# The first MLP's second projection: eight of its sixteen blocks in three rounded products instead of full-precision ones

## The reference, cut to what matters

```python
# first layer, behind its mixer; D_MODEL = 1024, D_FF = 4096
h = _rmsnorm(x, norm_g[0, 1]) * (1.0 + scale_f) + shift_f
x = x + gate_f * (jnp.square(jax.nn.relu(h @ w_fc1[0])) @ w_fc2[0])
# second layer: norm, then the S5 mixer (a linear state-space recurrence
# whose kernels come from lam, log_step, b, c), its gated projections, its MLP
```

## Time and profile before

| | us |
|---|---|
| median of 3 runs | 1177.98 |
| lowest and highest run | 1172.93, 1179.79 |
| span of the profiled execution (first to last instruction) | 1171.0 |
| PE busy in it | 1112.6 (95%) |
| DVE busy | 816.0 (70%) |
| ACT busy | 557.7 (48%) |
| `fc2_0` in it, first to last product | 306.7 to 443.3 |

### The profile page before, as it was taken

One profiled execution on the slowest core, in us unless ns is written; L12 is line 12 of the kernel. 1 busy time (PEld: TensorE's weight loads), 2 busy tenths in 40 slices (PEclk: granted clock), 3 DMA queues, 4 the chain that ended last, 5 costly groups with the idle time before them and its releaser, 6 DMA issues.

```text
span 1171.0 us, 22089 instructions
## 1 busy us (share of the span) xinstructions
PE 1112.6 (95%) x9466; PEld 995.9 (85%) x9466; DVE 816.0 (70%) x1390; ACT 557.7 (48%) x876; POOL 44.6 (4%) x71
## 2 busy tenths in 40 slices
PE   6899898999999997879999999999999999999998
PEld 4778686988888885469999999999988899988898
DVE  1599466877578674875666654478899966659955
ACT  3224633445111124554555543356568846467944
POOL 0010001000000000000000000000000000042000
PEclk8999999999999998999999999989989999999999
DMA  9887688899848957865355555525433345343342
GB/s 369 356 280 269 250 323 315 305 339 328 335 182 258 342 186 165 323 245 184 140 184 182 183 189 185 187 81 180 145 109 114 130 153 177 131 153 117 108 145 72
DMA packets 38290, 246.46 MB, mean 210 GB/s; under 512 B 4400, under 2 KB 5584, under 8 KB 9648
## 3 DMA queue, kind: packets, MB, share of 16 engines
q1 hardware_dynamic: 29072, 182.36, 45.7%
q0 software_dynamic: 6240, 43.94, 10.0%
q10 hardware_dynamic: 2880, 18.74, 3.9%
HBM read 225.24 MB, written 19.79 MB: 209 GB/s over the span
## 4 chain that ended last, share of the span: by engine, by line
PE 78%; DVE 10%; DMA 5%; ACT 5%; issue 2%; SPq 0%; ACTq 0%; DVEq 0%
PE ps L1452 16%; PE ps L1454 15%; PE ps L1456 15%; PE ps L1459 10%; PE ps L1555 4%; DMA ca_dram<-more 2%; PE ps L1648 1%; PE ps L1528 1%; PE ps L2083 1%; PE ps L1601 1%; PE ps L1539 1%; PE ps L1534 1%; DMA more<-in_ada_w 1%; DVE ring_rounded L2229 1%; DMA ada_more<-in_ada_w 1%
## 5 line engine op out<-in xcount | busy, mean ns | idle before, releaser
L1452 PE MATMUL ps<-sq_rounded,w_high_rounded 128*128 128x256 f32 x1184 | 341.6, 288 | 2.5 <-DVE mixT_rounded L2236 1.3
L1456 PE MATMUL ps<-sq_rounded,ring_rounded 128*128 128x256 f32 x1184 | 336.2, 284 | 0.0
L2229 DVE TENSOR_TENSOR ring_rounded<-ring,w_high_rounded 128x1024 fp32r<-128x1024 f32 x220 | 260.6, 1226 | 92.1 <-ACT w_high_rounded L844 91.8
L1454 PE MATMUL ps<-hT_rounded,w_high_rounded 128*128 128x256 f32 x992 | 282.1, 284 | 0.0
L844 ACT ACTIVATE w_high_rounded<-ring 128x1024 fp32r<-128x1024 f32 x220 | 219.8, 1049 | 67.0 <-PE ps L1456 66.3
L1452 PEld LDWEIGHTS ps<-sq_rounded,w_high_rounded 128*128 128x128 f32 x1184 | 228.5, 193 | 11.0 <-issue 6.7
L1456 PEld LDWEIGHTS ps<-sq_rounded,ring_rounded 128*128 128x128 f32 x1184 | 228.6, 193 | 0.0
L1454 PEld LDWEIGHTS ps<-hT_rounded,w_high_rounded 128*128 128x128 f32 x992 | 191.8, 193 | 0.1
L1452 PE MATMUL ps<-more_rounded,w_high_rounded 128*128 128x256 f32 x448 | 127.4, 284 | 0.4 <-issue 0.3
L1456 PE MATMUL ps<-more_rounded,ring_rounded 128*128 128x256 f32 x448 | 126.8, 283 | 0.0
L1459 PE MATMUL ps<-big,ring 128*128 128x256 f32 x544 | 121.0, 381 | 0.0
(11 more groups left out here) (426 smaller groups left out, 1640.3 us busy)
## 6 DMA issues: line engine op xcount, KB each, us to landing
ring<-in_blocks SPq DMA_DIRECT2D x139, 1024.0 KB, 4.9
ada_w<-in_ada_w POOLq DMA_DIRECT2D x27, 1024.0 KB, 7.7
ada_more<-in_ada_w POOLq DMA_DIRECT2D x13, 1024.0 KB, 7.6
we_dram<-we_t ACTq DMA_DIRECT2D x8, 1024.0 KB, 8.3
ca_dram<-more ACTq DMA_DIRECT2D x8, 1024.0 KB, 11.9
ring<-we_dram SPq DMA_DIRECT2D x8, 1024.0 KB, 5.5
ring<-ca_dram SPq DMA_DIRECT2D x8, 1024.0 KB, 6.8
big<-in_ada_w SPq DMA_DIRECT2D x4, 1024.0 KB, 10.9
```

The costliest lines, as they stand in the source:

```text
L1452: nc.tensor.matmul(out, high[:, k, columns], x_high, start=start, stop=False, skip_group_check=True)
L1454: nc.tensor.matmul(out, high[:, k, columns], x_low, start=False, stop=False, skip_group_check=True)
L1456: last = nc.tensor.matmul(out, low[:, k, columns], x_high, start=False, stop=stop, skip_group_check=True)
L2229: nc.vector.tensor_tensor(rounded(w), w, w_high[:, c % 2, ks], ALU.subtract)\
```

## The change

Blocks k = 0 and 1 of every output unit become split blocks, and the first unit takes its blocks in the order k = 2, 3, 0, 1, so the split ones are j = 2, 3, 4, 5, 8, 9, 12, 13. ACT rounds the first 16 tiles of `hid` (eight activations of 128x512) and the eight blocks; DVE makes the rest of both. Since `w_high` is now used until block 13, the loads of the first two near tables move from SP to ACT, behind three of the four squares of the next norm. The diff, cut to its core:

```diff
-    phase("fc2_0", [("fc2_0", k, n) for n in range(4) for k in range(4)])
+    phase("fc2_0", [("fc2_0", k, n) for n in range(4) for k in FC2_ORDER[n]])
...
+FC2_ORDER = ((2, 3, 0, 1), (0, 1, 2, 3), (0, 1, 2, 3), (0, 1, 2, 3))
+FC2_ROUND_BEHIND = {3: 4, 4: 5, 5: 6, 7: 8}
+FC2_SPLIT = tuple(4 * n + i for n in range(4) for i in range(4) if FC2_ORDER[n][i] < 2)
...
         def hid0_high(t, count):
+            return (sq if t < DT else hT)[:, t % DT:t % DT + count]
...
             def load_near(n):            # SP's
                 sp.wait_ge(k_stored, 16 * (n + 1))
-                if n >= 2:
-                    sp.wait_ge(near_here[n - 2], 16 * L)
+                sp.wait_ge(near_here[n - 2], 16 * L)
...
-                if b in NEAR_AT:
-                    load_near(NEAR_AT.index(b))
...
+            def load_near(n):            # ACT's
+                act.wait_ge(blocks_done, first_block["fc2_0"] + FC2_SPLIT[n - 2] + 1)
+                for j in range(L):
+                    act.dma_start(s5_near[n][GC * j:GC * j + GC], ...).then_inc(near_here[n], 16)
...
+            for t in range(8):                                   # ACT, behind fc1_0
+                act.wait_ge(hid_ready, t + 1)
+                round_tiles(hid0_high(2 * t, 2), hid[:, 2 * t:2 * t + 2])
+            round_to(first_block["fc2_0"] + FC2_SPLIT[1] + 1)
             store_kernels(1)
             store_outputs(2)
             for m in range(3, 8):
...
                 copy_weights(m, (0, 1, 2, 3))
                 store_weights(m)
+                if m == 3:
+                    round_to(first_block["fc2_0"] + FC2_SPLIT[2] + 1)
                 store_kernels(m - 1)
                 store_outputs(m)
+                if m in FC2_ROUND_BEHIND:
+                    round_to(first_block["fc2_0"] + FC2_SPLIT[FC2_ROUND_BEHIND[m] - 1] + 1)
...
-            norm_stats(2, 2)
+            log_and_exp()
+            act.wait_ge(blocks_done, first_block["fc2_0"] + FC2_SPLIT[-2] + 1)
+            for p in range(3):
+                square(2, 2, p)
+            load_near(0)
+            load_near(1)
+            square(2, 2, 3)
+            norm_rstd(2)
...
             for n in range(4):                                   # PE
-                project_deep("fc2_0", n, 4, (hid,), ..., after_block)
+                project_deep("fc2_0", n, 4, hid_tile, hid_arrived, after_block, FC2_ORDER[n])
...
             s5_outputs(2)                                        # DVE
+            for t in range(8):
+                lower_tiles("fc2_0", t, hid[:, 2 * t:2 * t + 2], hid0_high(2 * t, 2))
+            lower_to(first_block["fc2_0"] + FC2_SPLIT[1] + 1)
             for m in range(3, 8):
                 s5_weights(m)
+                if m == 3:
+                    lower_next()
                 s5_outputs(m)
+                if m in (3, 4, 5):
+                    lower_next()
                 if m in (4, 6):
                     residual("fc2_0", gate_f, m // 2 - 2, m // 2 - 1)
+            lower_to(first_block["fc2_0"] + FC2_SPLIT[7] + 1)
             residual("fc2_0", gate_f, 2, 3)
             s5_kernels(7)
```

More of the change, by code:

```diff
@@ L198 @@
 W_OUT_SPLIT = (1, 2)
+FC2_ORDER = ((2, 3, 0, 1), (0, 1, 2, 3), (0, 1, 2, 3), (0, 1, 2, 3))
+FC2_ROUND_BEHIND = {3: 4, 4: 5, 5: 6, 7: 8}
+FC2_SPLIT = tuple(4 * n + i for n in range(4) for i in range(4) if FC2_ORDER[n][i] < 2)
 TOGETHER = 2
 QUARTERS = 4
-SPLIT_LO = {"w_in": "vector", "w_out": "vector", "fc1_0": "vector", "glu": "vector", "fc1_1": "vector", "fc2_1": "vector", "xbc": "vector", "z": "vector",
+SPLIT_LO = {"w_in": "vector", "w_out": "vector", "fc1_0": "vector", "fc2_0": "vector", "glu": "vector", "fc1_1": "vector", "fc2_1": "vector", "xbc": "vector", "z": "vector",
             "ssm_out": "vector", "ple_gate_0": "vector", "q": "vector", "gate": "vector",
             "attn_out": "vector", "ple_gate_1": "vector"}
-SPLIT_SETS = (("w_in", 8), ("w_out", 8), ("fc1_0", 8), ("glu", 4), ("fc1_1", 8), ("fc2_1", 16), ("xbc", 8), ("ssm_out", 16), ("ple_gate_0", 8), ("q", 8),
+SPLIT_SETS = (("w_in", 8), ("w_out", 8), ("fc1_0", 8), ("fc2_0", 8), ("glu", 4), ("fc1_1", 8), ("fc2_1", 16), ("xbc", 8), ("ssm_out", 16), ("ple_gate_0", 8), ("q", 8),
               ("attn_out", 8), ("ple_gate_1", 8))
@@ L223, in split_plan @@
         for b in range(start, end) if name in SPLIT_LO else ():
-            if b - start not in {"w_in": W_IN_SPLIT, "w_out": W_OUT_SPLIT}.get(name, range(end - start)):
+            if b - start not in {"w_in": W_IN_SPLIT, "w_out": W_OUT_SPLIT, "fc2_0": FC2_SPLIT}.get(name, range(end - start)):
                 continue
@@ L236, in program @@
     laid_out = {b: i for i, b in enumerate(from_inputs(plan))}
-    NEAR_AT = (first_block["fc2_0"] + 10, first_block["fc2_0"] + 11)
     ctx = ExitStack()
@@ L636, in program, with hid0_high @@
         head_sq2, at = carve(ada_w_flat, at, 4, T)
+        def hid0_high(t, count):
+            return (sq if t < DT else hT)[:, t % DT:t % DT + count]
         hid_high, _ = carve(more, 0, FT, T)
@@ L895, in norm_squares @@
                     square(i, version, p)
+            def load_near(n):
+                act.wait_ge(blocks_done, first_block["fc2_0"] + FC2_SPLIT[n - 2] + 1)
+                for j in range(L):
+                    act.dma_start(s5_near[n][GC * j:GC * j + GC],
+                                  k_dram[n].rearrange("(q c) x a -> c q (x a)", q=4)
+                                  [0:GC, :, 4 * (L - 1 - j) * GC:4 * (L - 1 - j) * GC + 4 * P]).then_inc(near_here[n], 16)
             def norm_rstd(i):
@@ L1500, in project_tokens, with project_deep @@
                 last.then_inc(blocks_done, 1)
-            def project_deep(phase, n, kblocks, x, arrived=None, after=None):
+            def project_deep(phase, n, kblocks, tile, arrived=None, after=None, order=range(4)):
                 ps = pair(start_unit(phase, n))
-                for kb in range(kblocks):
-                    block_products(phase, n * kblocks + kb,
+                for j, kb in enumerate(order):
+                    block_products(phase, n * kblocks + j,
                                    (lambda k: arrived(kb * KB + k)) if n == 0 and arrived else None,
-                                   [(k, ps[:, i], slice(P * i, P * i + P), at_tile(x, kb * KB + k),
-                                     kb == 0 and k == 0 and i == 0, kb == kblocks - 1 and k == KB - 1)
+                                   [(k, ps[:, i], slice(P * i, P * i + P), tile(kb * KB + k),
+                                     j == 0 and k == 0 and i == 0, j == kblocks - 1 and k == KB - 1)
                                     for k in range(KB) for i in range(2)])
                     if after:
-                        after(n * kblocks + kb)
+                        after(n * kblocks + j)
             def swept(phase, n, unit=None):
@@ L1837, in after_block, with hid_tile, hid_arrived @@
                     s5_kernels(S5_KERNEL_AT.index(16 + j))
+            def hid_tile(t):
+                if t < 2 * KB:
+                    return rounded(hid0_high(t, 1)[:, 0]), rounded(hid[:, t])
+                return hid[:, t]
+            def hid_arrived(t):
+                if t % 2:
+                    return
+                if t < 2 * KB:
+                    pe.wait_ge(a_low, SET_BASE["fc2_0"] + t // 2 + 1)
+                else:
+                    pe.wait_ge(hid_ready, t // 2 + 1)
             for n in range(4):
-                project_deep("fc2_0", n, 4, (hid,), lambda k: pe.wait_ge(hid_ready, k // 2 + 1) if k % 2 == 0 else None,
-                             after_block)
+                project_deep("fc2_0", n, 4, hid_tile, hid_arrived, after_block, FC2_ORDER[n])
             norm_stats(2)
@@ L1956, in _ @@
             for n in range(4):
-                project_deep("fc2_1", n, 4, (hid_high, hid), split_arrived("fc2_1", 2))
+                project_deep("fc2_1", n, 4, lambda t: at_tile((hid_high, hid), t), split_arrived("fc2_1", 2))
             two_norm_stats()
```

## The result

The changed kernel takes **1193.96 us** (median of 4 runs, 1190.66 to 1197.53) where the kernel before, run beside it, takes 1177.18 (4 runs, 1172.93 to 1179.79). The ratio is 1.0157, with a 95% interval of 1.0131 to 1.0183: slower by some 17 us. The profiled execution took 1190.66 us with a span of 1188.7, against 1171.0 before, so the two traces differ by 17.7 us, close to the 16.8 between the medians.

A forecast was written before the change was run, and what follows sets the result against it. The prediction saw two chains ending within half a microsecond: PE's products, and DVE's S5 tables followed by the angles. Delays of 20.2 + 1 + 1 = 22 us on 1177.98 gave 1200, range 1188 to 1211.

The forecast's parts named there:

- Steps 1 and 2: DVE's start, then its wait for ACT to round block 4: outputs of group 3 13.5 us late, from 337.9.
- Step 3: DVE's list through groups 3 to 7, three lowerings at 3.9 each: outputs of group 7 end at 423.5, 9.6 late.
- Step 4: DVE lowers blocks 12 and 13 ahead of the last residual and kernel copies: 14.6 late, angles end at 457.4.
- Step 5: ACT issues 16 near transfers between third and fourth square, 7.7 us: fourth square 20.2 late.
- Step 6: Bounds without own rows: store of group 6, 1 us (0 to 13); near loads around the norm, 1 (-5.3 to +6).
- the bound of -5.3: Step 6's lower bound for near loads around the norm: PE's idle there falls away.
- Rival B: Smaller: near issues at their lower bound and PE's idle behind the norm gone, 14 us, 1192; chance 0.16.
- Rival A: Not slower: DVE's idle takes in 24.4 us, outputs of group 3 still start at 324.36; 1178.5; chance 0.07.
- C: Larger: stores near 15 us, or near loads holding up PE and the ring; 33 us, 1211; chance 0.17.

The follow-up runs named there:

- outputs_first: Changed kernel, but DVE makes the outputs of group 3 before the lowering that waits for ACT's rounding: 1188.56 us, ratio 1.0117 to the kernel before.
- eighth_lowered: Changed kernel with DVE's weight subtractions in the second projection cut to an eighth of their columns, all waits kept: 1188.41 us, ratio 1.0114 to the kernel before.
- near_behind: Changed kernel plus a wait that keeps ACT's 16 near transfers until its three squares have ended: 1197.37 us, ratio 1.0182 to the kernel before.
- warm_norm: Changed kernel with 13 idle products on PE ahead of the norm's sum of squares: 1195.64 us, ratio 1.0184 to the kernel before.
- near_sp: Changed kernel with the first two near tables loaded by SP instead of ACT, so the last two come earlier too: 1187.76 us, ratio 1.0111 to the kernel before.
- before_near: Kernel before, with SP loading the last two near tables one and two S5 blocks earlier: 1167.23 us, ratio 0.9933 to the kernel before.

## Why the prediction was right, and where it was not

The time lies inside the range, on the side that was forecast: 1193.96 against 1200, by the steps that the prediction names for its first 14.6 us. Behind these it is in part luck: a cost of 5.6 us that did not arise and one of 2.6 that the prediction had left out go against each other.

- **Steps 1 and 2, DVE's wait ahead of group 3: right.** Predicted 13.5 us late, at 337.9; it is 338.13, and the releaser is ACT's rounding (L846, the old L844). PE's idle there was to be some 7 us and is 7.09. outputs_first shows it as cause: without this order 7.7 us come back.
- **Step 3, DVE in one piece: right.** The outputs of group 7 were to end at 423.5 and end at 423.08 (421.85 and 1.23). Each lowering was put at 3.9 and takes 3.91. This step counted waits for ACT and subtractions together; eighth_lowered shows that only 1.13 of the 3.91 go when the subtraction shrinks to an eighth.
- **Step 4: right.** The last angle instruction was to end at 457.4 and ends at 457.44. PE's last product was put near 451.6 (its own terms give 451.4) and ends at 452.34. The fourth square is 14.6 us later than before, which is the sum up to here.
- **Step 5, the near issues: wrong in place, right in price.** The step said that ACT issues 16 transfers between its third and its fourth square for 7.7 us, so that the fourth comes 20.2 late instead of 14.6. The issues take 7.6 us (450.16 to 457.77) but run ahead of the squares they stand behind in the code, under the last long activations; they cost 0 in place of 5.6. near_behind, where a wait forces the order that the step assumed, pays 5.45 at the fourth square.
- **A step that is missing: the norm's sum at half clock.** The prediction has PE waiting several us for the norm, and gave that no price. After 5.97 us of idle the sum ran at a granted 0.50 and took 5.46 us against 2.83 before: 2.6 us later. warm_norm shows it as cause of these 2.6, and that the total does not gain when they go.
- **Step 6, the two bounds: 1 and 1 taken, 0 and 0.6 measured.** The stores did not hold DVE up at all; in the same stretch they land sooner than in the earlier trace rows (transfers issued from 340 to 430 us):

```profile
ca_dram<-more ACTq DMA_DIRECT2D x5, 1024.0 KB, 4.1
```

  The idle behind the norm went from 5.27 to 3.98, and PE's waits for the ring from 1.5 to 2.3 us (1.66 and 0.67). near_sp and before_near show that this stretch holds 8 us which the near loads cost in both kernels, so the bound of -5.3 in the prediction was a real chance; in the changed kernel the near tables still moved beside PE's load of instructions, and the idle stayed.

In all, the span was predicted 22 us longer and is 17.7: less 5.6 (step 5), less 1 and 0.4 (step 6), plus 2.6 (clock), which leaves 17.6. The other 1.7 us of the 6.0 between 1200 and 1193.96 are the runs around the profiled one: the median lay 7.0 above its span before, and 5.3 after.

On issue times the Trainium skill (DMA: Bandwidth & Descriptors, Issuing engines are not separate DMA queues) says that several issuing engines save only sequencer time, usually small against the transfer. Here the two are alike in length, 7.6 us of issue beside a median of 9.4 us to landing in the changed kernel. By that rule the near issues add next to nothing to the end, and that came true in the changed kernel, since other work of ACT lay beside them; with the wait of near_behind the fourth square came 5.45 us later. The prediction says that the sum would then stand at 14.6; with its two terms of step 6 that is 16.6, nearer to the 17.7 measured than its 22, and it gave this way no chance of its own.

Rival B named 1192, near the result, but on two grounds, cheaper issues and an idle that falls away. The idle did not fall away, and the issues were free, not cheaper. Rival A fell at the point it named: the outputs of group 3 started at 338 and not at 324.36. C's late stores did not show.

## What to carry to other kernels

A cheaper product pays nothing while a second chain ends beside it: look at what releases the next stage, then place the added work in that engine's list so that nothing waits on another engine ahead of work that is ready (one place here was worth 7.7 us). A transfer that stands behind an activation in the code need not be issued behind it: only a wait makes that order, for better or worse. And where a norm or another serial stretch follows, look at which loads still move beside it, by when they land and not by when they are issued: moving two tables away from it made the kernel before 0.7% faster, and no split kernel here is faster than that beyond the scatter.

## What the runs showed of the hardware that was not expected

ACT's queue issued 16 transfers from 450.16 on, while the three squares ahead of them in the code ran from 455.16 to 456.83. So the sentence ahead of the prediction that an engine works through its list in order does not hold between an engine's issues and its activations. These issues cost no time there; forced behind the squares, they took 7.48 us in which ACT computed nothing. The granted clock fell to 0.50 behind 5.97 us without products and doubled one stretch (5.46 us against 2.83); behind 13 idle products it stayed at 1.00 (2.86 us). And PE stood up to 7.25 us behind the norm until 1.3 to 1.7 us after a 16 KB load of instructions had ended, in ten kernels whose near tables still moved 7 us and more behind the norm's first activation, and not at all in near_sp and before_near, where they had moved 5 us behind it; how the one delays the other is open.
